# Three Strassen blocks instead of two in each feed-forward of a two-layer encoder trunk, with one weight sum made by an adding DMA and eight joins on ScalarE

## The reference, cut to what matters

```
x: (256 tokens, 1024) float32      w_gate, w_up: (1024, 2816)      w_down: (2816, 1024)
def _swiglu(h, w_gate, w_up, w_down):
    return (jax.nn.silu(h @ w_gate) * (h @ w_up)) @ w_down
x = x + 0.5 * _swiglu(_rms_norm(x, ffn_norm), w_gate, w_up, w_down)
```

## Time and profile before

| | |
|---|---|
| median of 3 (lowest, highest) | 1025.47 us (1024.95, 1027.05) |
| profiled execution | 1025.66 us |
| its span, first to last instruction | 1023.9 us |
| TensorE (PE) busy | 1018.2 us, 99% |
| VectorE (DVE) busy | 846.4 us, 83% |
| ScalarE (ACT) busy | 660.8 us, 65% |
| GpSimd (POOL) busy | 330.8 us, 32% |
| chain of waits, share of the span | PE 98%, ACT 1%, DVE 1% |
| read from HBM | 192.9 MB, 189 GB/s over the span |

### The profile page before, as it was taken

How to read it: one execution, slowest core, us unless ns; L and a number is a source line. 1 busy time by engine, 2 the same in 40 slices (tenths; PEclk the granted TensorE clock), 3 DMA queues, 4 the chain that set the end, 5 groups by cost and what they waited for, 6 DMA issues and landing times.

```text
span 1023.9 us, 13331 instructions
## 1 busy us (share of the span) xinstructions
PE 1018.2 (99%) x4905; PEld 853.9 (83%) x4905; DVE 846.4 (83%) x1008; ACT 660.8 (65%) x836; POOL 330.8 (32%) x258
## 2 busy tenths in 40 slices
PE   9999999999999999999999999999999999999998
PEld 6888888998888888888888888889988888888887
DVE  6999977698976898888679889866999678988972
ACT  6767665576874575766557666647778556666761
POOL 2999400138850100000049990001589300000000
PEclk9999999999999999999999999999999999999999
DMA  8968578555544596748749574975366365947491
GB/s 278 309 191 277 162 209 274 160 185 176 207 161 128 182 328 183 244 140 234 228 154 339 166 226 135 274 248 174 127 214 226 123 173 185 331 140 233 158 240 42
DMA packets 175185, 208.99 MB, mean 204 GB/s; under 512 B 64112, under 2 KB 129936, under 8 KB 175120
## 3 DMA queue, kind: packets, MB, share of 16 engines
q1 hardware_dynamic: 173904, 206.03, 64.9%
q10 hardware_dynamic: 1216, 2.11, 0.7%
HBM read 192.90 MB, written 1.05 MB: 189 GB/s over the span
## 4 chain that ended last, share of the span: by engine, by line
PE 98%; ACT 1%; DVE 1%; DMA 0%; issue 0%; POOL 0%; ACTq 0%
PE bank L829 30%; PE bank L831 30%; PE bank L830 30%; PE bank L966 1%; PE bank L1128 1%; PE bank L1137 1%; PE bank L1158 1%; PE bank L868 0%; PE bank L1136 0%; PE bank L1160 0%; PE bank L836 0%; DMA cacc<-in_ffn_norm 0%; DVE htok L1902 0%; DVE x L1950 0%; ACT htok L1357 0%; PE bank L1146 0%
## 5 line engine op out<-in xcount | busy, mean ns | idle before, releaser
L1854 DVE TENSOR_TENSOR wlo<-raw,whi 128x2048 fp32r<-128x2048 f32 (+2 forms) x136 | 308.9, 2283 | 21.0 <-ACT whi L1344 21.0
L1344 ACT ACTIVATE whi<-raw 128x2048 fp32r<-128x2048 f32 (+2 forms) x160 | 302.9, 1910 | 25.3 <-DMA raw<-in_ffn_w_down 16.5
L829 PE MATMUL bank<-whi,hThi 128*128 128x512 f32 (+1 forms) x816 | 316.1, 387 | 0.0
L831 PE MATMUL bank<-whi,hTlo 128*128 128x512 f32 (+1 forms) x816 | 311.4, 382 | 0.0
L830 PE MATMUL bank<-wlo,hThi 128*128 128x512 f32 (+1 forms) x816 | 311.3, 381 | 0.0
L697 POOL TENSOR_TENSOR small<-small,expo 128x1 f32<-128x1 f32 (+3 forms) x20 | 30.0, 1505 | 470.5 <-DVE small L1895 432.9
L831 PEld LDWEIGHTS bank<-whi,hTlo 128*128 128x128 f32 x816 | 153.2, 188 | 29.6
L829 PEld LDWEIGHTS bank<-whi,hThi 128*128 128x128 f32 x816 | 153.3, 188 | 28.8
L830 PEld LDWEIGHTS bank<-wlo,hThi 128*128 128x128 f32 x816 | 153.4, 188 | 28.4
L829 PE MATMUL bank<-whi,gThi 128*128 128x512 f32 (+1 forms) x416 | 162.3, 390 | 0.0
L831 PE MATMUL bank<-whi,gTlo 128*128 128x512 f32 (+1 forms) x416 | 161.2, 388 | 0.0
(11 more groups left out here) (201 smaller groups left out, 1359.0 us busy)
## 6 DMA issues: line engine op xcount, KB each, us to landing
raw<-in_ffn_w_down SPq DMA_DIRECT2D x88, 512.0 KB, 4.7
raw<-in_ffn_w_gate SPq DMA_DIRECT2D x68, 512.0 KB, 4.2
raw<-in_ffn_w_up SPq DMA_DIRECT2D x68, 512.0 KB, 5.2
raw<-in_w_in SPq DMA_DIRECT2D x48, 512.0 KB, 4.9
htok<-in_ffn_w_gate SPq DMA_DIRECT2D x16, 512.0 KB, 6.1
heads<-in_ffn_w_up SPq DMA_DIRECT2D x16, 512.0 KB, 6.8
raw<-in_w_out SPq DMA_DIRECT2D x16, 512.0 KB, 4.6
raw<-in_w_in SPq DMA_DIRECT2D x8, 544.0 KB, 5.2
```

The costliest lines, as they stand in the source:

```text
L829: nc.tensor.matmul(out, lh, rh, start=start, stop=False, skip_group_check=skip)
L831: return nc.tensor.matmul(out, ll, rh, start=False, stop=stop, skip_group_check=skip)
L1344: nc.scalar.activation(whi[:, slot(u, RING), 0:USED[u]], src, ACT.Copy).then_inc(whi_ready, 1)
L1854: nc.vector.tensor_tensor(wlo[:, slot(u, RING), 0:n], src, whi[:, slot(u, RING), 0:n].bitcast(F32), ALU.subtract).then_inc(wlo_ready, 1)
```

## The change

- The blocks stand at chunks 2, 5 and 8; plain chunks are 0, 1, 4, 7 and 10. TensorE's order is: chunks 0 and 1; strassen(2); pair(4); strassen(5); pair(7); strassen(8); last.
- T3 is no longer added by VectorE. GpSimd issues a DMA that adds the raw B22, as it lies in SBUF, to chain[1] in SBUF, once for each block. It waits for the raw unit, for chain[1] and for T1's sum. SP's next load into that raw slot waits for this sum.
- Joins of chunks 0 to 7 go from VectorE to ScalarE (`act_join`); those of chunks 8 and 9 stay.
- The orders of SP, ScalarE and VectorE are written anew around it.

```diff
-BLK = (4, 7)
+BLK = (2, 5, 8)
-SUM = {"T1": 1, "T2": 1, "T3": 1, "T4": 1}
+SUM = {"T1": 1, "T2": 1, "T3": 16, "T4": 1}
@@ SP
+                down(l, f, 0)
+                chain_load(l, f, 2, 0)
+                chain_load(l, f, 2, 1)
                 turn(0)
+                lower_load(l, f, 2, "B22")
+                lower_load(l, f, 2, "B21")
                 down(l, f, 1)
+                gate_up(l, f, 4, 0)
                 turn(1)
...
@@ POOL
+            def add_rows(l, f, c, name, lower):
+                done = per_block(l, f, c)
+                u = unit_block(f, c, lower)
+                pool.wait_ge(raw_landed[raw_slot(l, u)], raw_count(l, u))
+                if name == "T3":
+                    pool.wait_ge(chain_landed[1], done * 32)
+                    pool.wait_ge(sum_ready["T1"], done)
+                    dst = chain[1]
+                nc.gpsimd.dma_start(dst, raw[:, raw_slot(l, u), 0:2048], accum_op=ALU.add).then_inc(sum_ready[name], 16)
+            def first_sums(l, f):
+                add_rows(l, f, 2, "T3", "B22")
+            def second_sums(l, f):
+                add_rows(l, f, 5, "T3", "B22")
+            def third_sums(l, f):
+                add_rows(l, f, 8, "T3", "B22")
             for l in range(DEPTH):
                 norm(l, 0)
+                first_sums(l, 0)
...
                 turns(K2, two_pi)
                 for part in parts:
                     less(K2, part)
+                second_sums(l, 0)
                 less(KH, parts_big[3])
...
                 assert rstep[0] == N_ROPE
+                third_sums(l, 0)
                 norm(l, 1)
...
                 norm(l, 2)
+                first_sums(l, 1)
+                second_sums(l, 1)
+                third_sums(l, 1)
@@ TensorE
-                pair(2)
-                pair(3)
-                strassen(4)
-                pair(6)
-                strassen(7)
-                pair(9)
+                strassen(2)
+                pair(4)
+                strassen(5)
+                pair(7)
+                strassen(8)
                 last()
@@ ScalarE
+                def act_join(c):
+                    act.wait_ge(turned_landed, per_turn(l, f, c) * 16)
+                    if c:
+                        act.wait_ge(glo, per_ffn(l, f, c - 1, 1))
+                    nc.scalar.activation(g_turned.bitcast(U16).rearrange("p (n b) -> p b n", b=2),
+                                         turned.rearrange("p (b j) r -> p b (j r)", b=2), ACT.Copy).then_inc(joined, 1)
...
                 split_planes(0, 0)
+                first_of(2, "B11")
+                silu(1, 0)
                 split_planes(0, 1)
                 down_split(0)
+                sum_of(2, "T1")
+                act_join(0)
                 round_joined(0)
                 mixed_round()
+                silu(1, 1)
+                sum_of(2, "T2")
+                lower(2, "B22")
...
@@ VectorE
                 whole_rows()
                 if (l, f) != (0, 0):
                     gate_split(1, 0)
+                    norm_scale(l, 2 * f, 1)
+                    mul(0, 0)
                     gate_split(1, 1)
+                    mul(0, 1)
                 mixed_rows()
+                of_chain(2, "B11")
+                add_T1(2)
                 down_split(0)
+                of_chain(2, "T1")
+                rest_joined(0)
+                add_T2(2)
                 mul(1, 0)
                 mul(1, 1)
                 mixed_rest()
+                of_chain(2, "T2")
+                lower(2, "B22")
+                lower(2, "B21")
+                add_T4(2)
+                of_chain(2, "T3")
+                of_chain(2, "T4")
                 down_split(1)
...
```

More of the change, by code:

```diff
@@ L2151, in ffn @@
-                add_T1(7)
-                rest_joined(4)
+                mul(4, 0)
+                of_chain(5, "T2")
+                mul(4, 1)
+                lower(5, "B22")
+                add_T4(5)
+                lower(5, "B21")
+                of_chain(5, "T3")
+                of_chain(5, "T4")
+                rest_joined(4)
+                down_split(4)
+                gate_first(5)
+                gate_split(7, 0)
+                up_first(5)
+                gate_split(7, 1)
@@ L2153, in ffn @@
+                up_second(5)
+                gate_second(5)
+                block_mul(5, 0)
+                block_mul(5, 1)
                 down_split(5)
[L2154 to L2157 removed]
+                of_chain(8, "B11")
+                add_T1(8)
                 rest_joined(5)
[L2159 to L2163 removed]
```

261 lines of the change are left out of this document (112 added, 149 removed).

## The result

The changed kernel took 1054.54 us in the median of four executions (1052.23 to 1065.15), the kernel before beside it 1025.34: 1.0301 times the time, with a 95% interval of 1.0249 to 1.0354. That is slower, as forecast, but by 29 us where 14 were forecast, and outside the range. The profiled execution took 1054.08 us, 1052.3 of them between its first and last instruction.

A forecast was written before the change was run, and what follows sets the result against it. TensorE's instruction count times its pace was taken as the bound. 1025.66 - 10.9 (matmuls removed) + 11.0 (starts) + 1.6 (ends) + 12.6 (GpSimd's chain) = 1040.0, so 1039.8 us in the median; range 1024.5 to 1050.

The forecast's parts named there:

- in the middle there is room: From T4 of block 2 to T4 of block 5, VectorE has 39.4 us of work against TensorE's 46.2 us.
- GpSimd's chain: First feed-forward of each layer: block 5's sum, behind GpSimd's angles, stalls TensorE at T3 by 6.8 and 5.8 us.
- What is removed, 10.9 us: One more pair of chunks as a block: 84 matmuls for 96 in four feed-forwards, 10.9 us off TensorE's path.
- Starts, 4.7 + 3 x 2.1 = 11.0: TensorE stalls for VectorE at down(0): 4.7 us in the first feed-forward, 2.1 in each other; floor 7.7 in all.
- A join on ScalarE 1.06 us: Joins moved to ScalarE cost 1.06 us each; its load goes from 65% to about 75%, hidden behind TensorE.
- Ends, 1.6: End of each feed-forward: two turns one behind the other run late by some 0.4 us; total between 0 and 6.
- The adding DMA, 7 us: Each adding DMA takes 7 us, between 3.1 and 16; in block 2 it has 13.5 us of room, no cost.
- waits in the middle of the second feed-forwards: Sign named in advance: if TensorE's waits stand there in the changed profile, the prediction is wrong.
- Rival (4), the clock: TensorE falls to 1.2 GHz behind the three long stops: up to 16 us, 1056; one of three, 1045. Chance 0.07.
- Rival (1): GpSimd's chain to the second sums takes 54 us or less, so it is in time: 1027.2 us. Chance 0.23.
- (2): Faster: GpSimd in time, starts at their floor, no cost at the ends: 1022.3, down to 1014.6 us. Chance 0.11.
- (3): The adding DMA takes 16 us, making block 2 late in all four feed-forwards, block 5 in two: 1068. Chance 0.09.

The follow-up runs named there:

- without the mixing: Kernel with the adding DMA in block 2 alone, the mixing of activations on VectorE cut to one column: 1036.54 us, against 1039.02.
- with the order changed: Adding DMA in block 2 alone, matmuls on zeros and five moved instructions; at the starts chunk 0's join, rounding and remainder moved ahead of T1's: 1048.99 us.
- with two blocks: The kernel before, with the joins of chunks 0 to 7 moved to ScalarE and nothing else: 1025.62 us, ratio 1.000.
- the second trace: The changed kernel run and profiled once more, nothing altered: 1058.73 us (1.0320).
- Holding the DMA: Changed kernel, block 5's adding DMA in the second feed-forwards issued only once chunk 3's transposes have landed: 1052.20 us, against 1058.73 without the wait.
- The exchange on ScalarE: Changed kernel with the copy of T1's product put ahead of the rounding of T3 in ScalarE's list for block 5: 1057.54 us (1.0312).
- the filler: Kernel with the adding DMA in block 2 alone, plus 16 matmuls on zeros ahead of the first feed-forward's down(0): 1035.96 us, against 1039.02.
- the one with all repairs but layer 0's: Changed kernel plus matmuls on zeros, block 5's DMA held (not in the first feed-forward) and earlier in layer 1, ScalarE's T1 copy before T3's rounding: 1046.51 us.

## Why the prediction was wrong

In the prediction's terms the sum is 1040.0 and the measured one 1054.1. The 14.1 us between them are 6.0 of low clock behind stops, 4.8 of stops at down(3) in the second feed-forwards and 5.4 of stops too small to price one by one, less 1.4 at the starts, 0.6 at the ends and 0.1 at GpSimd's chain. So two steps failed for the size: the clock, which the sum took at nothing although its own stops were the condition for it, and "in the middle there is room". The step that failed as a mechanism, GpSimd's chain, gave nearly the right number by luck: 12.6 us forecast in two nearly equal parts, 12.5 measured in two very unequal ones.

- *What is removed, 10.9 us*: right. 48 matmuls fewer, pace unchanged between stops.
- *Starts, 4.7 + 3 x 2.1 = 11.0*: right in place and nearly in size: 4.3 and 3 x 1.5 to 1.6 idle, 9.6 counted as steps. The reason, "VectorE is the bound of this stretch whatever the order", is half of it: without the mixing the stops stay, held by the row behind B11's landing, and with the order changed they move to T1.
- *A join on ScalarE 1.06 us*: 1.36; with two blocks it did no harm. ScalarE's share rose to 69%; the working's own +16 us for each feed-forward give 70, not the 75 it names.
- *Ends, 1.6*: 1.0 once, nothing else over 0.3 us. Within its bounds.
- *The adding DMA, 7 us*: 7.1 where GpSimd was late, 9.3 in the median of the twelve. Right where it was used, and block 2 never waited for it.
- *"In the middle there is room"*: the first step that failed for the size. It counted VectorE's and TensorE's instructions and let the transposes keep their 3.1 us. Those of chunk 3, issued beside the 1 MB adding DMA, took 7 to 12 us, and down(3) waited: 1.9 + 3.0 us, 6.1 + 3.6 in the second trace. Holding the DMA shows it. The prediction had named waits in the middle of the second feed-forwards as a sign that it is wrong.
- *GpSimd's chain, 6.8 + 5.8 us*: failed as a mechanism, in both directions. From the first sum to the second the walk had 61.7 us in layer 0, where it took 53.5 and cost 1.7 us at most, and 59 in layer 1, where it took 60.4. The prediction expected a pace no better than before; in layer 0 it was. In layer 1 the start of the chain was right relative to TensorE. What I left out is what waits on ScalarE behind the sum: I named T4, the join and the down, and not the two copies that free B22's and T3's banks. So TensorE stood from B22 on, two products (5.4 us) before T3: 10.6 us, not 5.8. Against T3 itself, VectorE's remainder at 623.05 and a need at 615.9 would have been 7.2. The exchange on ScalarE moved the stop by these two products, as this says, but didn't shorten it.
- *Rival (4), the clock*, at 0.07: the second step that failed for the size. It came with the likeliest case and not in its place. Behind stops of 4.3, 10.6 and 2.8 us the matmuls ran at 1.2 GHz for 2.3, 2.0 and 1.7 us of loss, 6.0 in all. It was priced as an alternative to the forecast where the forecast's own stops were its condition; the filler shows that without the stop's idling the clock stays. The rule of the Trainium skill given there, "TensorE: Matmul & The Clock Gate", section "What's actually happening", agrees with these three stops; behind those of 1.5 to 1.7 us the clock stayed.
- *Rival (1)*, GpSimd in time, was half true: for one layer. *(2)* and *(3)* are excluded.

The sum with the measured terms: 1025.7 - 10.9 + 9.6 (starts) + 10.8 (layer 1) + 1.7 (layer 0, at down(5) and down(3)) + 4.8 (down(3), second feed-forwards) + 6.0 (clock) + 1.0 (turn) + 5.4 (small stops, in the mixer too) = 1054.1. The last term is what is left over, and its causes stay open. What the layer 0 chain would do was not decided by its instructions alone: from issue to issue it took 53 to 54 us in four traces of the changed kernel and its nearest kin, and 61.8 in the one with all repairs but layer 0's. Why, no run here shows.

## What to carry to other kernels

A wait added to an engine that works in order costs what stands behind it: list every instruction queued there, the copies that free a bank too, and price the stop from the first one that TensorE needs. Where a stall is forecast on TensorE, its clock belongs to the same case: add the matmuls behind the stop at half pace, or fill the stop. A long transfer put ahead of a short one on which a chain depends can lengthen the short one; before adding it, look in the timelines for what is issued within a microsecond or so of it, and in which order.

## What the runs showed of the hardware

- The transposes of one chunk, which landed in 3.1 us with little beside them, took 8.5 to 9.7 us when issued 0.5 to 1.2 us behind a 1 MB adding DMA from SBUF to SBUF, and 5.2 to 11.8 when issued 0.1 us ahead of it. When issued 0.4 us ahead they mostly took 4.5 to 5.1, and with the DMA held back 3.3 and 4.2. In the kernel before, which has no such DMA, five took 7.0 to 8.1 us too, and TensorE didn't wait for them. By the Trainium skill, "DMA: Bandwidth & Descriptors", section "Queues, rings and completion order", each DMA engine takes turns between its rings packet by packet; that this is the reason no run here shows.
- The adding DMA of 1 MB took 7.1 us where it came late in the changed kernel's chains of angles, and 8.0 to 14.9 us elsewhere in its two traces.
- TensorE's granted clock fell to 1.2 GHz behind stops of 2.8, 4.3 and 10.6 us, stayed at 2.4 GHz behind stops of 1.7 us, and behind a stretch of 4.2 us of which matmuls on zeros filled 3.4. In the other kernels it fell once behind a stop of 2.0 us, and of the stops of 2.1 to 3.2 us some lowered it and some didn't.
- A remainder on GpSimd took 5.55 us, and a VectorE instruction beside it 6.0 in place of 2.28.
